# Compression of mixers 2 and 3 with the token blocks as fixed operand, and its items dealt between the projection items

## What is computed

```python
def compress(k, pos, w1, b1, w2, b2):
    blocks = k.reshape(bsz, g, s // CMP_STRIDE, CMP_STRIDE, dh)
    win = jnp.concatenate([blocks[:, :, r:r + n_cmp] for r in range(ratio)], axis=3)
    win = (win + pos).reshape(bsz, g, n_cmp, CMP_BLOCK * dh)
    return jax.nn.gelu(win @ w1 + b1) @ w2 + b2

def hybrid_mixer(h, w_in, cmp_pos, cmp_w1, cmp_b1, cmp_w2, cmp_b2, conv_w, w_o):
    z = h @ w_in
    q, kc, vc, ks, vs, kw, vw, gates, u, bg, cg = jnp.split(z, offsets, axis=-1)
    kc_c = compress(kv(kc), cmp_pos[0], cmp_w1[0], cmp_b1[0], cmp_w2[0], cmp_b2[0])
    vc_c = compress(kv(vc), cmp_pos[1], cmp_w1[1], cmp_b1[1], cmp_w2[1], cmp_b2[1])
    o_cmp, p_cmp = cmp_attention(q, kc_c, vc_c)
    ...
    o_conv = short_conv(u, bg, cg, conv_w)
    return jnp.concatenate([o_attn, o_conv], axis=-1) @ w_o
```

## Time and profile before

| | before |
|---|---|
| median of 3 runs | 2536.1 us (2535.78 to 2538.53) |
| profiled execution, span | 2541.9 us (no time of its own is given) |
| TensorE busy | 2485.4 us, 98% |
| VectorE busy | 1400.3 us, 55% |
| ScalarE busy | 1004.8 us, 40% |
| GpSimd busy | 198.0 us, 8% |
| mean granted TensorE clock | 0.991 |

### The profile page before, as it was taken

One profiled execution on the slowest core, in us unless ns is written; L12 is line 12 of the kernel. 1 busy time (PEld: TensorE's weight loads), 2 busy tenths in 40 slices (PEclk: granted clock), 3 DMA queues, 4 the chain that ended last, 5 costly groups with the idle time before them and its releaser, 6 DMA issues.

```text
span 2541.9 us, 37934 instructions
## 1 busy us (share of the span) xinstructions
PE 2485.4 (98%) x15206; PEld 2007.3 (79%) x15206; DVE 1400.3 (55%) x2055; ACT 1004.8 (40%) x1379; POOL 198.0 (8%) x161
## 2 busy tenths in 40 slices
PE   7999999999999999999999999999998999999997
PEld 6888888887788887877778888878675888888885
DVE  5433445576543345667463323466756666766676
ACT  4222233345422222346342222234543555555552
POOL 1000010010100002200030000220002000000000
PEclk9999999999999999999999999999998999999999
DMA  4221223212222232321122323222114777777783
GB/s 156 102 111 70 106 91 116 85 37 71 91 101 106 83 112 71 114 97 34 67 81 89 112 83 107 91 95 100 51 44 185 267 278 270 290 272 274 275 317 124
DMA packets 52614, 332.13 MB, mean 131 GB/s; under 512 B 6688, under 2 KB 6816, under 8 KB 21024
## 3 DMA queue, kind: packets, MB, share of 16 engines
q1 hardware_dynamic: 45184, 310.60, 33.7%
q0 software_dynamic: 5888, 17.55, 2.1%
q10 hardware_dynamic: 1440, 2.57, 0.3%
HBM read 317.19 MB, written 12.98 MB: 130 GB/s over the span
## 4 chain that ended last, share of the span: by engine, by line
PE 90%; DVE 5%; ACT 2%; DMA 2%; issue 1%; POOL 0%; ACTq 0%; DVEq 0%; SPq 0%; POOLq 0%
PE ps L2538 17%; PE ps L2540 17%; PE ps L2539 17%; PE ps L950 5%; PE ps L1608 3%; PE ps L1592 3%; PE ps L1609 3%; PE ps L1610 3%; PE ps L431 2%; PE ps L1647 2%; PE ps L1648 2%; PE ps L1649 1%; PE ps L1004 1%; PE ps L1634 1%; PE ps L1039 1%; PE ps L1019 1%
## 5 line engine op out<-in xcount | busy, mean ns | idle before, releaser
L2538 PE MATMUL ps<-xh,wh 128*128 128x512 f32 x1232 | 482.0, 391 | 14.3 <-DVE wl L2491 11.8
L2540 PE MATMUL ps<-xh,wl 128*128 128x512 f32 x1232 | 480.1, 390 | 0.0
L2539 PE MATMUL ps<-xl,wh 128*128 128x512 f32 x1232 | 480.0, 390 | 0.0
L1877 DVE TENSOR_TENSOR wml<-raw_m,wmh 128x2048 fp32r<-128x2048 f32 (+1 forms) x144 | 302.3, 2109 | 146.6 <-ACT wmh L1725 146.4
L2054 ACT CAST wh<-raw 128x2048 fp32r<-128x2048 f32 (+4 forms) x126 | 251.1, 1992 | 321.3 <-PE ps L2540 292.0
L2059 DVE TENSOR_TENSOR wl<-raw,wh 128x2048 fp32r<-128x2048 f32 (+4 forms) x126 | 306.4, 2432 | 120.9 <-ACT wh L2054 120.7
L1725 ACT CAST wmh<-raw_m 128x2048 fp32r<-128x2048 f32 (+1 forms) x144 | 254.8, 1771 | 197.8 <-PE ps L1592 113.8
L2538 PEld LDWEIGHTS ps<-xh,wh 128*128 128x128 f32 x1232 | 231.8, 188 | 66.1 <-DVE wl L2491 12.3
L2540 PEld LDWEIGHTS ps<-xh,wl 128*128 128x128 f32 x1232 | 231.7, 188 | 48.5
L2539 PEld LDWEIGHTS ps<-xl,wh 128*128 128x128 f32 x1232 | 231.8, 188 | 48.2 <-issue 0.5
L2538 PE MATMUL ps<-ah,wh 128*128 128x512 f32 x528 | 206.2, 391 | 0.0
(11 more groups left out here) (423 smaller groups left out, 4195.2 us busy)
## 6 DMA issues: line engine op xcount, KB each, us to landing
raw_m<-in_moe SPq DMA_DIRECT2D x104, 1024.0 KB, 6.0
raw<-in_ffn_up SPq DMA_DIRECT2D x65, 1024.0 KB, 4.8
raw_m<-in_moe SPq DMA_DIRECT2D x32, 768.0 KB, 4.7
raw<-in_in SPq DMA_DIRECT2D x20, 1024.0 KB, 4.9
raw<-in_ffn_down SPq DMA_DIRECT2D x12, 1536.0 KB, 6.6
raw<-in_ffn_down SPq DMA_DIRECT2D x12, 1280.0 KB, 5.4
raw<-in_cmp SPq DMA_DIRECT2D x8, 1024.0 KB, 4.8
raw<-in_out SPq DMA_DIRECT2D x8, 1024.0 KB, 4.8
```

Source lines behind the costliest of these rows:

```text
L1877: nc.vector.tensor_tensor(wml[:, n % SPLITS, cols], raw_m[:, n % RAWS, cols], wmh[:, n % SPLITS, cols].bitcast(F32), ALU.subtract).then_in ...
L2538: nc.tensor.matmul(dst, hi_w, hi_x, start=(k == 0), stop=False)
L2539: nc.tensor.matmul(dst, hi_w, lo_x, start=False, stop=False)
L2540: return nc.tensor.matmul(dst, lo_w, hi_x, start=False, stop=(k == last_k))
```

## The change

In `MIXER_ITEMS` the nine items get the order in0, in1, tok, cmp0, in2, cmp1, in3, cmp2, cmp3. SyncE's loads, ScalarE's casts, VectorE's low parts and PE follow it. Compression turns its operands: the 124 window columns (62 high, 62 low) of a chunk are the fixed operand, and a weight block of 128 x 256 moves, so an item has 8 chunks x 2 parts = 16 matmuls, and the result has windows as rows, in one bank. VectorE copies these 124 x 256 numbers into `hidtok`. A join then multiplies them with a 124 x 62 table of ones (new columns of `cmpw`), which adds high and low rows and turns the result back; two fp32 matmuls for kv = 0 in the middle of in3, two for kv = 1 in the middle of the first convolution half. ScalarE's gelu reads PSUM and adds the bias. The items in2, in3, cmp3 and the first convolution item are split in halves. The banks are dealt anew (`item_bank`): tok takes near to near + 3, and in0 near and near + 1. The filler columns of `win` and their memset (L1190) go.

```diff
+MIXER_ITEMS = ("in0", "in1", "tok", "cmp0", "in2", "cmp1", "in3", "cmp2", "cmp3")
...
-        stage(f"in{l}", [ITEM] * 4)
-        stage(f"tok{l}", [KD * 280])
-        stage(f"cmp{l}", [ITEM] * 4)
+        stage(f"in{l}", [KD * 280 if name == "tok" else ITEM for name in MIXER_ITEMS])
...
-                cmpw = sb("cmpw", [P, 480], on=mid2)
+                cmpw = sb("cmpw", [P, 480 + 2 * NCMP], on=mid2)
...
-                    win = sb("win", [P, 2, 16 * WIN + WIDE - WIN], F32R, on=win_scope)
+                    win = sb("win", [P, 2, 16 * WIN], F32R, on=win_scope)
+                    hidtok = sb("hidtok", [WIN, 2, 256], on=win_scope)
...
+        join = cmpw[0:WIN, 480:480 + 2 * NCMP]
...
+        def item_bank(l, name):
+
+            near = 4 * (first[f"in{l}"] % 2)
+            far = 4 - near
+            return {"in0": near, "in1": far, "tok": near, "cmp0": far + 2, "cmp1": far + 2, "in2": far, "in3": near + 2,
+                    "cmp2": far + 3, "cmp3": far + 3, "join0": near + 1, "join1": far + 2}[name]
...
-            for j in range(4):
-                n, kv = n0 + j, j // 2
-                slot = n % 2
-                pe.wait_ge(d_lo, 2 * l + kv + 1)
-                pe.wait_ge(d_window, 2 * l + 2)
-                pe.wait_ge(lo_ready, n + 1)
-                for hh in range(2):
-                    for c in range(8):
-                        cols = slice(c * 256 + hh * P, c * 256 + hh * P + P)
-                        at = (8 * (j % 2) + c) * WIN
-                        x2 = win[:, kv, at:at + WIDE]
-                        dst = ps[:, hidden_bank(l) + 2 * kv + hh, 0:WIDE]
-                        nc.tensor.matmul(dst, wh[:, slot, cols], x2, start=(j % 2 == 0 and c == 0), stop=False)
-                        mm = nc.tensor.matmul(dst, wl[:, slot, cols], x2, start=False, stop=(j % 2 == 1 and c == 7))
-                mm.then_inc(item_done, 1)
-
-            pe.wait_ge(evac_done, n0 + 2)
-            conv(0, 0, 24)
+            conv(0, 0, 12)
+            hidden_join(l + 1, 1)
+            conv(0, 12, 24)
             pe.wait_ge(d_gelu, 2 * l + 2)
+            pe.wait_ge(evac_done, mixer_item(l + 1, "in3") + 1)
...
+            whole("tok")
+            for kv in range(2):
+                act.wait_ge(d_window, 2 * l + kv + 1)
+                nc.scalar.copy(windows(kv)[:, :, 0], wnf.rearrange("p c g n -> p c (g n)")).then_inc(d_hi, 1)
+            heads_hi("in1", qh[:, 0:2])
+            whole("cmp0")
+            by_halves(mixer_item(l + 1, "in2"))
+            whole("cmp1")
...
+            by_halves(mixer_item(l + 1, "in3"))
+            heads_hi("in2", qh[:, 2:4])
+            whole("cmp2")
             gelu(0)
-            act_split(nb, nb % 2, nb // 2, ITEM)
+            by_halves(mixer_item(l + 1, "cmp3"))
+            by_halves(nb)
+            heads_hi("in3", kh[:])
             gelu(1)
...
+            def first_half_held(name):
+
+                n = mixer_item(l + 1, name)
+                dve.wait_ge(item_done, n + 1)
+                dve.wait_ge(evac_done, n)
+                dve.sem_inc(evac_done, 1)
+
+            def hidden_rows(kv):
+
+                name = f"cmp{2 * kv + 1}"
+                dve.wait_ge(item_done, mixer_item(l + 1, name) + 1)
+                nc.vector.tensor_copy(hidtok[:, kv], ps[0:WIN, item_bank(l + 1, name), 0:256]).then_inc(evac_done, 1)
...
+            heads_lo("in1", 1, ql[:, 0:2], qh[:, 0:2])
+            whole("cmp0")
+            by_halves("in2")
+            dve.wait_ge(item_done, mixer_item(l + 1, "tok") + 1)
+            at = item_bank(l + 1, "tok")
+            nc.vector.tensor_copy(vgate[:], ps[:, at:at + 4, 0:280]).then_inc(evac_done, 1)
+            first_half_held("cmp0")
+            whole("cmp1")
+            by_halves("in3")
+            heads_lo("in2", 2, ql[:, 2:4], qh[:, 2:4])
+            hidden_rows(0)
+            whole("cmp2")
             nc.vector.memset(vcz[:], 0.0)
             chain.then(nc.vector.memset(kcf[:], 0.0))
-            cmp_split(2)
-            hidden(0)
-            cmp_split(3)
-            dve_split(nb, nb % 2, nb // 2, ITEM)
-            hidden(1)
+            by_halves("cmp3")
+            by_halves("conv")
+            heads_lo("in3", 3, kl[:], kh[:])
+            first_half_held("cmp2")
+            hidden_rows(1)
...
+            def hidden_item(l, j):
+
+                name = f"cmp{j}"
+                n, kv = mixer_item(l, name), j // 2
+                slot, dst = n % 2, ps[0:WIN, item_bank(l, name), 0:256]
+                if name == "cmp3":
+                    pe.wait_ge(lo_first, half_lo(l, name))
+                else:
+                    pe.wait_ge(lo_ready, n + 1)
+                for c in range(8):
+                    if name == "cmp3" and c == 4:
+                        pe.wait_ge(lo_ready, n + 1)
+                    at = (8 * (j % 2) + c) * WIN
+                    cols = slice(c * 256, (c + 1) * 256)
+                    nc.tensor.matmul(dst, win[:, kv, at:at + WIN], wh[:, slot, cols], start=(j % 2 == 0 and c == 0), stop=False)
+                    mm = nc.tensor.matmul(dst, win[:, kv, at:at + WIN], wl[:, slot, cols], start=False, stop=(j % 2 == 1 and c == 7))
+                mm.then_inc(item_done, 1)
+
+            def hidden_join(l, kv):
+
+                pe.wait_ge(evac_done, mixer_item(l, f"cmp{2 * kv + 1}") + 1)
+                for hh in range(2):
+                    mm = nc.tensor.matmul(ps[:, item_bank(l, f"join{kv}"), hh * HD:hh * HD + 2 * NCMP],
+                                          hidtok[:, kv, hh * P:(hh + 1) * P], join, start=True, stop=True)
+                mm.then_inc(d_hidden, 1)
+
+            def in_items(l, norm):
+
+                in_item(l, "in0", split_base[norm])
+                pe.wait_ge(lo_first, FIRST_LOW[norm])
+                pe.wait_ge(evac_done, mixer_item(l, "in0"))
+                in_item(l, "in1")
+                pe.wait_ge(evac_done, mixer_item(l, "in0") + 1)
+                tokens(mixer_item(l, "tok"), 280)
+                pe.wait_ge(d_lo, 2 * l - 1)
+                pe.wait_ge(d_window, 2 * l)
+                hidden_item(l, 0)
+                pe.wait_ge(evac_done, mixer_item(l, "in1") + 1)
+                in_item(l, "in2")
+                hidden_item(l, 1)
+                pe.wait_ge(evac_done, mixer_item(l, "tok") + 1)
+                in_item(l, "in3")
+                pe.wait_ge(d_lo, 2 * l)
+                hidden_item(l, 2)
+                hidden_item(l, 3)
...
-                load_items(first[f"in{l + 1}"], 4, ITEM, t[f"in{l + 1}"][0:4])
-                load_items(first[f"tok{l + 1}"], 1, KD * 280, t[f"tok{l + 1}"])
-                load_items(first[f"cmp{l + 1}"], 4, ITEM, t[f"cmp{l + 1}"])
+                for name in MIXER_ITEMS:
+                    table, j = (t[f"tok{l + 1}"], 0) if name == "tok" else (t[f"{name[:-1]}{l + 1}"], int(name[-1]))
+                    load_items(mixer_item(l + 1, name), 1, KD * 280 if name == "tok" else ITEM, table[j:j + 1])
...
+        small[0:4 * NCMP, 480:480 + 2 * NCMP] = np.arange(4 * NCMP)[:, None] % (2 * NCMP) == np.arange(2 * NCMP)[None, :]
```

More of the change, by code:

```diff
@@ L901, in build @@
         pos = cmpw[:, 448:480].rearrange("p (v c) -> p v c", v=2)
+        join = cmpw[0:WIN, 480:480 + 2 * NCMP]
+        FIRST_LOW = {"ln_in": 2, "ln1_0": 7, "ln2_0": 8}
+        HALVES = {"in2": 0, "in3": 1, "cmp3": 2, "conv": 3}
         cs = raw[:, 0, ITEM:ITEM + 2 * 16 * NPAD].rearrange("p (g i c n) -> p g i c n", g=2, i=NT, c=4)
@@ L939, in conv @@
                     if x == 0:
-                        pe.wait_ge(lo_ready, n + 1)
+                        pe.wait_ge(lo_first, half_lo(l + 1, "conv")) if q == 0 else pe.wait_ge(lo_ready, n + 1)
                         if q >= 2 and m == 1:
@@ L1065, in act_mixer, with whole, by_halves @@
         def act_mixer(act, chain, l):
-            na, n0, nb = (first[f"{name}{l + 1}"] for name in ("in", "cmp", "conv"))
+            nb = first[f"conv{l + 1}"]
             base = split_base[f"mixed{l + 1}"]
             u0, t0 = STEPS1 + STEPS * l, NT * l
[L1069 to L1086, removed]
+            def whole(name):
+                n = mixer_item(l + 1, name)
+                act_split(n, n % 2, n // 2, sizes[n])
+            def by_halves(n):
                 act.wait_ge(raw_loaded[n % 2], (n // 2 + 1) * 16)
@@ L1233, in hidden @@
-            def hidden(kv):
-                n, bank = n0 + 2 * kv + 1, hidden_bank(l) + 2 * kv
-                dve.wait_ge(item_done, n)
-                dve.sem_inc(evac_done, 1)
-                dve.wait_ge(item_done, n + 1)
-                for hh in range(2):
-                    b1 = vec(f"cmp_b1{l}")[:, 2 * kv + hh:2 * kv + hh + 1]
-                    ins = nc.vector.tensor_scalar(hid[:, kv, hh], ps[:, bank + hh, 0:2 * NCMP], b1, None, ALU.add)
-                chain.then(ins)
-                for hh in range(2):
```

(40 more changed lines are left out.)

134 lines of the change are left out of this document (50 added, 84 removed).

## The result

The changed kernel takes 2545.1 us (median of 10 runs), the kernel before 2539.7 us beside it: a ratio of 1.0021, 95% interval 1.0013 to 1.0029. It is slower by 5.4 us, just at the edge of what can be told from no change. The forecast was a ratio of 2541.1 / 2536.1 = 1.0020. The profiled execution has a span of 2543.8 us, 1.9 above that of before.

A forecast was written before the change was run, and what follows sets the result against it. TensorE, busy for 98% of the span, was taken to bound the kernel. Savings paid back by gap, joins and waits left +0.4 us, clock falls +4.6: +5.0 on the 2536.1 median, 2541.1 us, range 2534.5 to 2545.5.

The forecast's parts named there:

- Saving: Compression on PE: 64 matmuls instead of 128 at 119 ns, 7.6 us less a mixer; old waits of 1.7 also go.
- rival 4: Compression: halved matmuls no cheaper, as swapped operands expose weight-load time; 4.4 us a mixer, 2550 us; chance 0.03.
- Gap: Before tok: PE waits for in0's evacuation count, behind the second window's cast; 4.83 us in mixer 2, 5.66 in mixer 3.
- the landing of cmpw: In the window chain: cmpw is 13% bigger and VectorE waits for it; 0 to 0.5 us later, 0.2 taken.
- Rival 2: Before tok: in0's banks come free before in1 ends, no gap; 5.0 us a mixer faster, 2526.0 us; chance 0.10.
- Waits and joins: Around short items: 0.85 us each before in2 and in3, 1.3 around cmp3, sum 3.1 a mixer; joins 0.58 each.
- Rival 3: Around short items: half splits slip or a compression load lands late; 1 to 3 us more a mixer; chance 0.11.
- Clock: In or behind the halt before tok: PE's clock falls to 0.5 in both mixers; 2.3 us each, +4.6.
- Rival 1: Before tok: the gap comes, but the clock holds or falls once; +0.4 to +2.7 us, 2536.5 to 2538.8; chance 0.18.
- one halt of 2.48 us: PE halt in the old profile, followed by 3.4 us at half clock; taken as evidence that longer halts bring falls.
- both old falls behind the key scores: Behind the key scores, one clock fall a mixer (3.4 and 6.7 us slow); said to stay, perhaps trading 1.6 for 3.1.
- Sum: Whole kernel: +0.4 us at full clock and +4.6 for the clock, +5.0 us in all, 2541.1 us.

The follow-up runs named there:

- experiment 7: Kernel before, with the position table resident and the wait for cmpw moved behind the windows' additions: 2538.0 us, ratio 0.9996 to the kernel before.
- experiment 1: Changed kernel, but tok writes to free banks 2, 3, 6 and 7 and only cmp0 waits for in0's banks: 2530.3 us, ratio 0.9962 to the kernel before.
- experiment 2: Changed kernel, banks kept, but position table resident and VectorE waiting for cmpw only after the windows: 2533.2 us, ratio 0.9972 to the kernel before.
- experiment 3: Changed kernel plus 22 matmuls of 512 columns, results unread, before the wait for in0's banks: 2539.9 us, ratio 1.0000 to the kernel before.
- experiment 4: Turned operands alone: changed kernel with items in the old order and banks so that tok waits for nobody: 2537.7 us, ratio 0.9992 to the kernel before.
- experiment 5: Changed kernel with tok in banks 2, 3, 6 and 7 and the position table resident: 2528.35 us, ratio 0.9955 to the kernel before.
- experiment 6: Changed kernel with each compression item's 16 matmuls issued twice, first into an unread bank: 2553.2 us, ratio 1.0053 to the kernel before.

## Why the prediction was right

**Saving.** 64 compression matmuls a mixer are gone. 15 steps from 1056.57 to 1058.34 give 118 ns each; 119 was assumed. 124 fixed columns and the turn change nothing in the pace, so rival 4 is out. The Trainium skill (TensorE: Matmul & The Clock Gate, Back-to-back issue gap) gives 109 ns for 256 columns by a formula that it calls the gap of an isolated matmul; the trace, whose matmuls each come with a weight load, again does not show that.

**Gap.** Predicted 4.83 and 5.66 us, measured 1042.20 - 1036.73 = 5.47 and 1689.38 - 1683.82 = 5.56. The mechanism and the releaser are those predicted. Mis-sized is the landing of cmpw, taken 0.2 us later than before. In mixer 2 VectorE's wait for it ends at 1029.92 before and at 1031.17 after; of these 1.25 us 0.37 is the whole stretch's shift, so the landing is 0.88 later, and the memset that is gone gives 0.28 back. In mixer 3 it is 1.49 (1676.86 to 1678.35) less 1.35 of shift, 0.14. From issue to landing (median of a trace's two) the table of 240 KB took 4.6 us in the kernel before and 4.5 in experiment 7, that of 271 KB 5.2 in the changed kernel and 5.0 to 5.8 in experiments 1 to 6. So the larger table lands 0.4 to 1.3 us later, not 0.2, and by how much differs from trace to trace. The sum over both gaps, 11.0 for 10.5, hides it: that is luck. The halt also hides tok's own split, which the prediction had at 1035.5: it ends at 1036.70 and is what experiment 1 then waits for. Rival 2 (no gap) was not what happened, but experiments 1, 2 and 5 show that its price was right: 5.0 us a mixer, 10.1 in all, was said for a head without gap, experiment 5 gained 0.0045 of 2540, 11.4 us (3.4 either way), and its trace shows 5.3 a mixer.

**Waits and joins.** Predicted 3.0 up to the convolution. Measured: 52.64 us (in1's end to 1089.37) less 5.47, 14.37, 7.6, 21.76 and 0.45 for the first join leave 3.0. In2 and in3 wait 0.81 after the last matmul's turn (1058.46 to 1059.27), and cmp2 to the convolution take 1.2 over their 3.8. A join costs 0.37 (1078.47 to 1078.84) and some 0.08 in the next matmul, 0.45 and not 0.58; the second one takes 0.44, with no halt in front of it. Rival 3 is out.

**Clock.** Predicted 2.3 us a mixer, measured 2.02 and 2.63: 4.65 for 4.6. Both falls came, and experiment 3 shows the halt as their cause: with the same order, and tok as late, but PE at work in between, the clock holds in both mixers. Experiments 1, 2 and 5, without the halt, have no fall there either. Rival 1 is out. That 2.3 was hit so closely is luck. It was a middle value between bounds of 0 and 3.1, and what a fall costs hangs on how much of the slow stretch lies in the halt; behind the halts of experiment 6 tok takes 13.75 and 14.91 us, which is 1.4 and 2.56 over 12.35. The prediction's step from one halt of 2.48 us that "was enough" is also weaker than it looked. The same halt, 2.4 to 2.8 us, stands near the end of all nine traces: a fall follows it in the kernel before and in experiments 2, 6 and 7, and none in the changed kernel (2.64) and in experiments 1, 3, 4 and 5 (up to 2.76). The halts of 5 us and more before tok, four in two traces, brought the clock down each time. The same page of the Trainium skill says in Why this matters for your kernels that halts between bursts bring the clock down; this trace agrees, for the halts of 5.31 and 5.40 us. The prediction also let both old falls behind the key scores stay; the changed kernel's trace has only the one of mixer 3.

**Sum.** +5.0 predicted, +5.1 in the two stretches, +5.4 by the runs (its interval is 3.3 to 7.4). That the runs come so near the two stretches rests on the other clock falls being as frequent in both kernels; in the two profiled executions they were not, and the spans differ by 1.9. The absolute medians stand higher than in the runs shown first, for both kernels (2539.7 for 2536.1), which is why the ratio is what counts.

## What to carry to other kernels

When items are reordered, ask of every item which banks it writes and who still reads them: an item with a free set of banks that gets one from its neighbour but two turns a late, harmless chain (a small table's load, two passes of VectorE, a cast) into a halt of the busiest engine. Count a halt of this length twice, once for itself and once for the clock behind it, and look whether the count that ends it is raised as soon as the banks are read. Halving a stream of matmuls on the busiest engine is worth only what the loads and splits of the next items can follow; put short items between long ones, and check the chain they now wait for.

## What was not expected of the hardware

The clock fell inside the halt, 3.0 us after the last matmul in mixer 2 and 4.4 in mixer 3, not when work began again. It stayed at 1.2 GHz for 6.8 us in both, of which the halt itself covered 2.5 and 1.2; the fall that started earlier in its halt cost less (2.02 against 2.63). In mixer 2 of experiment 6 the same kind of halt was followed by only 3.4 us at 1.2 GHz (1041.0 to 1044.3). In the token matmuls a slow stretch of 4.3 us cost 2.0 us.

The falls behind the key scores come and go. In the kernel before there were two. In experiment 7, the same but for a wait that nobody felt, the same matmuls ran at 1.00 (kernel before first, then experiment 7; windows of time):

```profile
1103.00:1107.00 4.00, 4.00 (x22) 3.23 (x21) 3.44 (x9) 0.43 (x3) 0.00 (x0) 0.62 0.01 4
1749.00:1756.00 7.00, 7.00 (x29) 5.72 (x28) 5.84 (x12) 1.82 (x5) 0.00 (x0) 0.51 0.01 2
```

```profile
1103.00:1107.00 4.00, 4.00 (x26) 3.31 (x25) 3.72 (x9) 0.72 (x4) 0.00 (x0) 1.00 0.02 4
1749.00:1756.00 7.00, 7.00 (x38) 5.25 (x37) 6.25 (x19) 3.32 (x11) 0.00 (x0) 1.00 0.00 0
```

The spans are 2541.9 and 2536.1. The two falls were priced at 1.6 and 3.1 us, most of that difference, and the runs of the kernel before alone range from 2535.8 to 2543.4. In the 38 of them that stand beside the experiments the time goes with the mean granted clock: 2536.1 to 2537.5 us at 0.995, 2537.5 to 2539.7 at 0.994, 2539.0 to 2542.4 at 0.993, 2542.3 and 2542.9 at 0.992. So this spread is, in the main, clock. That it is these two falls only the two traces suggest, and what decides whether such a fall comes stays open.
